# Block two's first columns and first weight panel move into the tail of block one; its constants and rotation tables move behind its first product

## What is computed

```python
def reference(x, positions, ..., c_2, positions_2, w_ada_2, b_ada_2, w_in_2, ...):
    x = first_block(x, positions, attn_norm_g, w_in, ..., w_down)
    return second_block(x, c_2, positions_2, w_ada_2, b_ada_2, w_in_2, ...)

# the end of first_block, for each of its two layers
    u = jax.nn.silu(h @ w_gate[l]) * (h @ w_up[l])
    x = x + u @ w_down[l]

# the start of second_block, for each of its two layers
    mod = cond @ w_ada[l] + b_ada[l]
    sh1, sc1, g1, sh2, sc2, g2 = split(mod, 6)
    h = x * (1.0 + sc1) + sh1
    y = _token_mixer(h, positions, lb_all[l], w_in[l], ...)   # p = h @ w_in; q, k are rotated by cos, sin of positions
```

## Time and profile before

| what | us |
|---|---|
| three timed runs, median | 3587.74 |
| their lowest and highest | 3586.67, 3592.58 |
| the profiled execution | 3599.51 |
| its span, first to last instruction | 3597.7 |

### The profile page before, as it was taken

The page is one execution under the profiler, slowest core; times in us unless marked ns, Lnnn a source line. Parts: engine busy times, 40 slices in busy tenths (PEclk is TensorE's granted clock), DMA queues, the critical chain, the costliest instruction groups (busy, mean ns, idle before and its releaser), DMA issues. The chain is left out here.

```text
span 3597.7 us, 38873 instructions
## 1 busy us (share of the span) xinstructions
PE 3363.6 (93%) x15296; PEld 2680.7 (75%) x15296; DVE 2138.4 (59%) x2733; ACT 1283.8 (36%) x1652; POOL 607.7 (17%) x495
## 2 busy tenths in 40 slices
PE   7899999999999999959988998999899979989997
PEld 5677788886678788847776886888677768868886
DVE  7754566448644765447985336554668864365545
ACT  4664322235653322223223324333432232243323
POOL 1122222121212211210000222010200002121002
PEclk9999999999999999979999999999999999999999
DMA  3122454321224544222211222222211112322221
GB/s 121 44 61 83 177 197 187 108 102 54 57 75 146 187 187 150 72 91 71 71 53 41 88 100 95 94 94 93 83 62 68 56 56 71 101 82 94 94 97 67
DMA packets 72182, 344.44 MB, mean 96 GB/s; under 512 B 25153, under 2 KB 26049, under 8 KB 35649
## 3 DMA queue, kind: packets, MB, share of 16 engines
q1 hardware_dynamic: 70560, 340.17, 27.1%
q0 software_dynamic: 432, 1.28, 0.2%
q10 hardware_dynamic: 1008, 0.51, 0.1%
HBM read 340.51 MB, written 2.10 MB: 95 GB/s over the span
## 5 line engine op out<-in xcount | busy, mean ns | idle before, releaser
L841 PE MATMUL bank_b<-Hhi_b,whi_b 128*128 128x512 f32 x2976 | 1228.9, 413 | 104.6 <-DVE wlo_b L819 51.9
L842 PE MATMUL bank_b<-Hhi_b,wlo_b 128*128 128x512 f32 x2976 | 1176.9, 395 | 0.0
L848 PE MATMUL bank_b<-Hlo_b,whi_b 128*128 128x512 f32 x2976 | 1166.9, 396 | 0.8 <-DVE Hlo_b L2225 0.8
L819 DVE TENSOR_TENSOR wlo_b<-raw_b,whi_b 128x2048 fp32r<-128x2048 f32 (+2 forms) x290 | 626.0, 2159 | 568.1 <-ACT whi_b L813 567.9
L841 PEld LDWEIGHTS bank_b<-Hhi_b,whi_b 128*128 128x128 f32 x2976 | 570.8, 192 | 256.8 <-issue 78.5
L842 PEld LDWEIGHTS bank_b<-Hhi_b,wlo_b 128*128 128x128 f32 x2976 | 570.8, 192 | 126.7 <-issue 14.2
L848 PEld LDWEIGHTS bank_b<-Hlo_b,whi_b 128*128 128x128 f32 x2976 | 567.5, 191 | 126.9 <-DVE Hlo_b L2225 4.0
L813 ACT ACTIVATE whi_b<-raw_b 128x2048 fp32r<-128x2048 f32 (+2 forms) x290 | 511.3, 1764 | 363.4 <-PE bank_b L848 363.4
L841 PE MATMUL bank_b<-Uhi_b,whi_b 128*128 128x512 f32 x1024 | 406.3, 397 | 0.0
L842 PE MATMUL bank_b<-Uhi_b,wlo_b 128*128 128x512 f32 x1024 | 398.7, 389 | 0.0
L848 PE MATMUL bank_b<-Ulo_b,whi_b 128*128 128x512 f32 x1024 | 385.2, 389 | 0.0
(11 more groups left out here) (249 smaller groups left out, 3471.2 us busy)
## 6 DMA issues: line engine op xcount, KB each, us to landing
raw_b<-in_w SPq DMA_DIRECT2D x234, 1024.0 KB, 4.9
ada_b<-in_wada SPq DMA_DIRECT2D x48, 1024.0 KB, 6.9
raw_b<-in_w SPq DMA_DIRECT2D x40, 512.0 KB, 3.6
raw_b<-in_w SPq DMA_DIRECT2D x16, 768.0 KB, 4.2
rel_b<-in_rel SPq DMA_DIRECT2D x128, 24.0 KB, 2.4
X_keep<-in_x SPq DMA_DIRECT2D x4, 512.0 KB, 8.6
out<-X_keep SPq DMA_DIRECT2D x8, 256.0 KB, 2.0
cond_b<-in_c SPq DMA_DIRECT2D x2, 512.0 KB, 4.6
```

The lines of the kernel that those rows point to most:

```text
L819: self.nc.vector.tensor_tensor(self.wlo[n % RAW_SLOTS][:, 0:words], self.raw[n % RAW_SLOTS][:, 0:words], self.whi[n % HI_SLOTS][:, 0:words ...
L841: self.nc.tensor.matmul(out, whi[:, k, cols], xhi, start=(k == 0), stop=False)
L842: self.nc.tensor.matmul(out, wlo[:, k, cols], xhi, start=False, stop=False)
L848: mm = self.nc.tensor.matmul(out, whi[:, k, cols], xlo, start=False, stop=(k == nk - 1))
```

## The change

`block_two` is now built before block one is written and hands out functions: `lead_load`, `lead_act`, `lead_dve` and `run`. Both blocks share the eight PSUM banks. Block one's last four products get a `column` hook that adds an item `lead` for each column of `X`; on it ACT and DVE do block two's column `h`. ACT makes `Hhi` from `X` directly (Identity with scale and bias), DVE makes `hf` and subtracts to `Hlo`; POOL has no part in it. At column 5 (`LEAD_SPLIT`) the split of block two's panel 0 goes in too: its `round` ahead of ACT's column 5, its `rest` behind DVE's column 5. SP loads block two's panels 0 and 1 at the end of block one. In block two the coefficients and the angles (`setup`) stand behind the first product, the sines behind the eviction of that product (`sines`), the angles have a fourth buffer, so that the second table does not share one with the first, and `decay` is loaded by POOL and has its wait at its first use. PE's wait for the constants is at the first `rrot`. With indentation left out (the body of `block_two` moved one level):

```diff
+LEAD_PANELS, LEAD_SPLIT = 2, 5
...
-n = ffn_stages(s, n, l, (lambda c: rms_chunk(s, l + 1, "attn", c)) if l + 1 < DEPTH else None, ada_panel,
-root=lambda: rms_root(s, l, "ffn"))
+n = ffn_stages(s, n, l, (lambda c: rms_chunk(s, l + 1, "attn", c)) if l + 1 < DEPTH else
+(lambda c: s.add("lead", c)), ada_panel, root=lambda: rms_root(s, l, "ffn"))
...
+s.load_ahead(LEAD_PANELS - RAW_SLOTS)
+s.lead_loads, s.loads, s.lead = s.loads, [], []
+for c in range(DC):
+if c == LEAD_SPLIT:
+s.round_next()
+s.temp("hf", 2, ("hf", 0, "mix", c))
+s.add("h", 0, "mix", c)
+if c == LEAD_SPLIT:
+s.rest_next()
+s.lead.append(s.items)
+s.items = []
 for l in range(DEPTH):
 s.add("pad", l)
 if l == 0:
 s.add("tables", 0)
-for k in range(DC):
-s.temp("hf", 2, ("hf", l, "mix", k))
-s.add("h", l, "mix", k)
...
+if l == 0 and i == 1:
+s.add("sines")
 if i == 0:
 s.product(n, nk, 256, cols, rhs, k_outer=True)
+if l == 0:
+s.add("setup")
...
 k.load_panels(sp, d["w1"], load_bias, load_cond, load_ada, load_x, load_masks)
+for n in range(LEAD_PANELS):
+sp.wait_ge(*after(*s.last_use[2 * PANELS1 - RAW_SLOTS + n]))
+two.lead_load(sp, n)
...
+elif kind == "lead":
+if a[0] == LEAD_SPLIT:
+act.wait_ge(*after(*s.last_use[2 * PANELS1 - HI_SLOTS]))
+act.wait_ge(*after("x", DEPTH, "attn", a[0]))
+two.lead_act(act, a[0])
...
+elif kind == "lead":
+dve.wait_ge(*after("x", DEPTH, "attn", a[0]))
+two.lead_dve(dve, a[0])
...
-tab_tmp = [tab.put(f"tab{i}", [P, SEQ]) for i in range(3)]
+tab_tmp = [tab.put(f"tab{i}", [P, SEQ]) for i in range(4)]
...
-loads = [(rot128[:], d["rot128"]), (vec[:], d["vec2"]), (invt[:], d["inv128"]),
-(pos_i[:], d["pos2"].partition_broadcast(P)), (decay[:], d["decay"])]
+loads = [(vec[:], d["vec2"]), (invt[:], d["inv128"]), (pos_i[:], d["pos2"].partition_broadcast(P)),
+(rot128[:], d["rot128"])]
...
+elif kind == "h":
+l, w, c = a
+act_e.activation(k.Hhi[:, c], X[:, c], ACT.Identity, bias=modcol(l, c), scale=modcol(l, 8 + c))\
+.then_inc(*mark("act", ("hi", "h", l, w, c)))
...
 elif kind == "h":

 l, w, c = a
+hf_c = buf(("hf", l, w, c))
 reuse(dve, ("hf", l, w, c))
-nv.tensor_scalar(buf(("hf", l, w, c)), X[:, c], modcol(l, 8 + c), modcol(l, c), ALU.mult,
-ALU.add).then_inc(*mark("dve", ("hf", l, w, c)))
+nv.tensor_scalar(hf_c, X[:, c], modcol(l, 8 + c), modcol(l, c), ALU.mult, ALU.add)\
+.then_inc(*mark("dve", ("hf", l, w, c)))
+dve.wait_ge(*after("hf", l, w, c))
+dve.wait_ge(*after("hi", "h", l, w, c))
+nv.tensor_tensor(k.Hlo[:, c], hf_c, k.Hhi[:, c].bitcast(F32), ALU.subtract)\
+.then_inc(*mark("dve", ("h", l, w, c), ("free", ("hf", l, w, c))))
...
-if l > 0 and h == 0:
-dve.wait_ge(table_landed, 16 + 32 * l)
+if h == 0:
+dve.wait_ge(table_landed, 32 * (l + 1))
...
-pe.wait_ge(const_landed, 16 * NCONST2)
...
+if l == 0 and h == 0 and t == "rq":
+pe.wait_ge(const_landed, 16 * NCONST2)
```

More of the change, by code:

```diff
@@ new lines, in sem @@
+    def sem(name):
+        return ctx.enter_context(nc.semaphore(name + "_2"))
+    sems = {e: sem(e + "_steps") for e in ("pe", "act", "dve", "pool")}
+    steps = Steps(sems, known)
+    landed = [sem(f"panel_landed{i}") for i in range(RAW_SLOTS)]
+    const_landed, table_landed, out_landed = sem("const_landed"), sem("table_landed"), sem("out_landed")
+    mem, keep, d, end = io["mem"]("b2"), io["keep"], io["dram"], io["end"]
+    k = Common(nc, "b2", s, steps, keep, mem, landed)
+    k.bank = banks
@@ new lines, in block_two @@
+    rot128 = mem.put("rot128", [P, P])
+    vec = mem.put("vec", [P, DEPTH, NV2])
+    lb, oml = mem.put("lb", [P, DEPTH, 4]), mem.put("oml", [P, DEPTH, 4])
+    coef = mem.put("coef", [P, 3, 4, 8])
+    idle_root = mem.put("idle_root", [P, 4])
+    mem.line()
+    ulow = mem.at
+    k.Uhi = mem.put("Uhi", [P, 12, SEQ], R32)
+    mem.at += 512
+    ulo_at = mem.at
+    k.Ulo = mem.put("Ulo", [P, 12, SEQ], R32)
+    cos, sin = mem.put("cos", [P, SEQ]), mem.put("sin", [P, SEQ])
+    area = mem.at
@@ new lines, in block_two @@
+    decay = mem.put("decay", [P, 4, SEQ])
+    yml = mem.again(area, mem.at)
+    k.ym = [yml.put(f"ym{i}", [P, SEQ]) for i in range(4)]
+    k.sg = [mem.put(f"sg{i}", [P, SEQ]) for i in range(2)]
+    k.mt = [mem.put(f"mt{i}", [P, SEQ]) for i in range(2)]
+    level = mem.put("level", [P, len(LEVELS), P], mybir.dt.uint8, size=1)
+    mem.line()
+    past_tables = mem.at
+    RQ, RK, VV, GG = ([mem.put(f"{n}{i}", [P, SEQ]) for i in range(2)] for n in ("RQ", "RK", "VV", "GG"))
+    FT = [mem.put(f"FT{i}", [P, SEQ]) for i in range(2)]
@@ new lines, in block_two @@
+    t2 = um.put("t2", [P, SEQ])
+    pos_i = um.put("pos_i", [P, SEQ], I32)
+    TL = mem.again(um.at - SEQ * 4, um.at).put("TL", [P, SEQ])
+    hf = [mem.again(ulow + i * SEQ * 4, ulow + (i + 1) * SEQ * 4).put(f"hf{i}", [P, SEQ]) for i in range(2)]
+    PAD = CONV_K - 1
+    Up = mem.again(ulow + 8 * SEQ * 4, ulo_at).put("Up", [P, 4, PAD + SEQ])
+    acc = mem.again(ulo_at + 8 * SEQ * 4, area).put("acc", [P, 4, SEQ])
+    lnb = mem.again(ulow + 8 * SEQ * 4, ulo_at)
+    qa, xa, sx, m2 = (lnb.put(n, [P, SEQ]) for n in ("qa", "xa", "sx", "m2"))
@@ new lines, in vcol, with modcol, normed, tile @@
+    def vcol(l, name, c=0):
+        j = V2[name] + c
+        return vec[:, l, j:j + 1]
+    def modcol(l, j):
+        return keep.mod[:, l, j:j + 1]
+    NORMS = {(0, "mix"): (0, "ln1", 0, 24), (0, "ffn"): (1, "ln2", 1, 0), (1, "mix"): (2, "ln1", 1, 24)}
+    def normed(l, w, part, c):
+        return coef[:, NORMS[l, w][0], part, c:c + 1]
+    def tile(t, n=1):
+        return slice(t * P, (t + n) * P)
+    def halves(ap, L):
+        return ap.rearrange("p (b two l) -> p b two l", two=2, l=L)
@@ new lines, in block_two, with totals, at_col, residual @@
+    tl_at, at = {}, 0
+    for L in LEVELS[1:] + (128,):
+        tl_at[L] = at
+        at += SEQ // L
+    def totals(l, h, L):
+        return buf(("FT", l, "h", h)) if L == 1 else TL[:, tl_at[L]:tl_at[L] + SEQ // L]
+    def at_col(j):
+        return (0, 512, 896, 1152)[j]
+    def residual(l, w, c):
+        if l == 0 and w == "mix":
+            nv.tensor_scalar(X[:, c], X[:, c], ALPHA, None, ALU.mult).then_inc(*mark("dve", ("scaled", l, w, c)))
+        else:
+            by = (l, "mix") if w == "ffn" else (l - 1, "ffn")
+            nv.tensor_scalar(X[:, c], X[:, c], normed(*by, 2, c), normed(*by, 3, c), ALU.mult, ALU.add)\
+                .then_inc(*mark("dve", ("scaled", l, w, c)))
@@ new lines, in shift_column, with sp_lead @@
+    def shift_column(dve, ready, l, w, c):
+        dve.wait_ge(*after(*ready))
+        dve.wait_ge(*after("mh", l, w))
+        names = [("free", ("mh", l, w))] if c == DC - 1 else []
+        nv.scalar_tensor_tensor(out=X[:, c], in0=k.out_of(("mh", l, w))[:], scalar=-2.0 / D, in1=X[:, c],
+                                op0=ALU.mult, op1=ALU.add).then_inc(*mark("dve", ("xs", l, w, c), *names))
+    def sp_lead(sp, n):
+        kind, src, words, panel = s.lead_loads[n]
+        sp.dma_start(k.raw[panel % RAW_SLOTS][:, 0:words], d["w2"][src, :, 0:words]).then_inc(landed[panel % RAW_SLOTS], 16)
@@ new lines, in sp_work @@
+    def sp_work(sp):
+        loads = [(vec[:], d["vec2"]), (invt[:], d["inv128"]), (pos_i[:], d["pos2"].partition_broadcast(P)),
+                 (rot128[:], d["rot128"])]
+        assert len(loads) == NCONST2
+        for dst, src in loads:
+            sp.dma_start(dst, src).then_inc(const_landed, 16)
+        k.load_panels(sp, d["w2"])
+        for c in range(DC):
+            sp.wait_ge(*after("xn", DEPTH - 1, "ffn", c))
+            sp.dma_start(d["out"][:, c], X[:, c]).then_inc(out_landed, 16)
+        sp.wait_ge(out_landed, 16 * DC)
@@ L2386, in block_two @@
-    return steps.found
+            pe_work(pe)
+        return steps.found
+    return BlockTwo(sp_lead, lambda act, c: act_work(act, s.lead[c]), lambda dve, c: dve_work(dve, s.lead[c]), run)
 def constants():
@@ L2519, in program @@
     io = dict(dram=d, keep=keep, end=end, mem=lambda tag: Map(nc, tag, low.at, end))
-    found1 = block_one(nc, io, known and known[0])
-    found2 = block_two(nc, io, known and known[1])
+    with ExitStack() as ctx:
+        banks = [ctx.enter_context(t) for t in psum_banks(nc)]
+        two = block_two(nc, io, known and known[1], banks, ctx)
+        found1 = block_one(nc, io, known and known[0], banks, two)
+        found2 = two.run()
     return found1, found2
```

1332 lines of the change are left out of this document (627 added, 705 removed), and 6 rows, old and new, of the table names.

## The result

| | median us | lowest and highest | runs |
|---|---|---|---|
| before, beside the changed kernel | 3590.16 | 3586.67, 3593.56 | 4 |
| changed | 3558.33 | 3556.70, 3564.79 | 4 |

The changed kernel takes 0.9915 of the time of before, with a 95% interval from 0.9898 to 0.9932. Of 3590.16 that is 30.5 us, between 24.4 and 36.6. The forecast was a gain of 37.0 us and a time of 3550.7, with a range up to 3556.5. The sign and the main part of the gain are right. The size is 6.5 us too large, and the measured median lies outside the range.

The account below looks back on a forecast made before the run. The prediction took PE's 38.62 us idle chain between the blocks as the bound. It summed 35.7 + 1.6 - 0.3 = 37.0 us, so 3587.74 - 37.0 = 3550.7 us, range 3546 to 3556.5.

Parts of the forecast that it names:

- What bounds the kernel: Between the blocks: PE idles 38.62 us behind a chain without PE work; all that leaves it shortens the kernel.
- Part 1: Block one's tail: with columns and first panel there, block two's first matmul starts 35.7 us earlier.
- Rival 3: PE's jump into block two: it begins 1.8 us later and the clock falls, 3554.1 to 3555.6 us; chance 0.07.
- Part 2: Block two's first matmuls: full clock after the short gap, gain 1.6 us, bounds +1.6 and -1.5.
- Rival 1: Between the blocks: PE's clock falls in the short gap, price 1.6 to 3.1 us; chance 0.25.
- Part 3: Block two behind its first product: constants, angles and split moved there make the third product wait 0.3 us.
- Rival 2: Block two's third product: panel 2 late, constants taking 9 us or more, price 2.4 to 4 us; chance 0.12.
- Rivals 4 and 5: 4: block one's splits delayed, work only moves, 3569 us, chance 0.02. 5: clock stays low in block two, 3625, chance 0.01.

Follow-up runs that it names:

- each half of the change alone: Changed kernel cut to columns and first panel in block one's tail (3570.89 us, 0.9948), or to constants and tables behind the first product (3572.90 us, 0.9952).
- early constants: Changed kernel with the four constants loaded in block one's tail, behind panel 0's load; 3548.78 us, 0.9897 of before.

## Why the prediction was right and where it failed

**What bounds the kernel: right.** All that left the chain of 38.62 us shortened the kernel, and each half of the change alone took about 20 us of M off it.

**Part 1, the tail: right to 0.3 us.** The sum gave 35.7 us, and the trace shows 35.4. The gap was 3.24 instead of 2.9. In each of the last two columns, which stand one behind the other on DVE, the hand-over from ACT to DVE took 0.37 and not 0.1, 0.54 us together, of which some 0.2 came back elsewhere in the chain: ACT rounds `X` with scale and bias in 0.81 us, not in the 0.61 of the old rounding. The row for that instruction was taken from another form of it. Block one's last two splits, which I had ending at 1515.6 and 1522.4, ended at 1509.94 and 1516.81 in a trace that runs 5.86 us ahead there, so at 1515.8 and 1522.7 by the clock of before, and PE had no gap in the last products. The jump cost PE 0.19 us (1530.70 to 1530.89) against the 0.2 taken. Rival 3 is out, and with it the stall that the Trainium skill ("Runtime: NRT & Kernel Launch", section "Instruction fetch mechanics") lets one fear; no trace here shows it.

**Part 2, the clock: right as a term, not as a certainty.** In the trace of after the 1.6 us came in full. Rival 1 had 0.25, and the clock fell at this place in 5 of 9 traces, so it deserved about a half. That it did not fall in the trace of after was luck. Its price was 1.7 us where nothing else was late (35.55 against 37.24), the lower end of what I gave. In the changed kernel itself it would have cost nothing, because panel 2 was later still.

**Part 3, what moved behind the first product: the step that failed.** It moved the constants' wait, the angles and the split of panel 2 behind the first product and said 6.6 us for the constants, 11.2 for the angles, panel 2 at 22.7 after the opening, and a wait of 0.3. Measured:

- *The constants' landing, 10.0 us instead of 6.6 (3.4 us).* The step took `pos_i`'s 5.3 us from a trace in which three panels were in flight, and counted one panel now as a relief. It gave the move of `decay` to POOL's queue the price of one issue on POOL. But on SP's queue `decay` had stood behind the four constants, and on POOL's queue it starts beside them. The change put 1 MB in their way, and then excused it since nobody reads `decay` early. With `decay` and `level` late they came at 5.35. The step also took `pos_i` for the last of the four, and it was `rot128`, issued behind it: of the 3.4 us, 1.0 is `pos_i` (landed 7.6 us after the meeting) and 2.4 the 64 KB behind it. No run leaves `rot128` out of DVE's wait, or keeps `decay` at the end of SP's queue. The Trainium skill says it in "DMA: Bandwidth & Descriptors", section "Issuing engines are not separate DMA queues": loads that different engines issue run on the same 16 DMA engines and interleave. By that rule a load moved to another queue still counts against its neighbours, and the landings of 8.6 and 4.0 us of the same 64 KB agree. Even the range for this number, 4 to 9.0, was too narrow at its upper end, and the upper end was measured with `decay` included.
- *DVE standing still, 2.0 us instead of nothing.* Two operations took 1.06 and 0.97 us more beside POOL's multiplications. The trace of before had shown this to me, in the row where `hf` takes 1476 ns at most and 540 in the median; I used the median. The Trainium skill ("SBUF — State Buffer", section "Who interferes with whom") says that DVE and GpSimd share a pair of ports exclusively for certain forms of DVE's instructions, and that the second to issue blocks fully. The traces agree: the excess is 0.97 to 1.06 us for an operation of either 0.43 or 0.69, and not in proportion to it, and in the trace with early constants an operation that DVE began 0.06 us before POOL's pair kept its 0.43 us, while the next took 1.40.
- *The clock behind the wait, 2.4 us instead of nothing.* I gave panel 2's delay its own length as price. A wait of 4.93 us let the clock fall too. After waits of 1.12 and 2.11 us at the same place the clock stayed up, and behind 2.55 us it fell for a while (the third product reached the score pair in 9.7 us after the two short ones, 11.3 after the third, 11.9 after 4.93).

With the first two panel 2 was ready 28.0 us after the opening instead of 22.7, 5.3 us later, and 3.4 + 2.0 = 5.4 of it is named. The wait grew by 4.6 and not by 5.3, because PE wanted the panel at 28.00 - 4.93 = 23.07 after the opening and not at 22.5. The rest of that step stands: coefficients and angles took 11.1 us (forecast 11.2) wherever DVE wasn't held up, and 72.46 - 37.0 = 35.46 us was the forecast for M, and with the constants out of the way it is 35.55 in two traces and 37.24 in a third, where the clock fell.

**Rival 2 was the case, with a chance of 0.12.** Its mechanism (constants compete with `decay` and a panel, and take 9 us or more) is what the runs show as far as POOL's two loads go; the panel's share is not measured, and its price of 2.4 to 4 was too small by the standing still and by the clock. The argument that I put against it compared the number of panels and left out when each load starts. Rivals 4 and 5 are out.

**The base.** The forecast was put on a median of 3587.74, and before took 3590.16 in four runs, including those three. That is 2.4 us of the 7.6 between 3550.7 and 3558.33, and no fault of a step.

## What to carry to other kernels

When a change moves a load to another engine's queue, ask first which loads it now starts beside, and only then who reads it: the queue's order had been a priority, and the move gives it up. Where several loads share one semaphore, the reader waits for the last of them, also for one that it doesn't read. Where an operation moves onto the critical path next to another engine's work, take its longest duration in the trace and not its median, if the trace has a collision in it. And price a new wait of PE with what the clock does behind it, not only with its own length; but where something else sets the time anyway, a cold start can be free.
